# A two-block MoE transformer on one core: folded norms, token-major first heads, and embedding products inside the expert stretch

## The reference, cut to what matters

```python
o = _rmsnorm(o, subln_g) * (1.0 - lambda_init)         # o: (B, S, 8 heads, 128), first mixer
x = x + g1 * (o.reshape(B, S, D) @ w_out)
# second block, per layer
x = layer_norm(DEEPNORM_ALPHA * x + mix @ w_o[i], ln1_g[i], ln1_b[i])
ffn = expert_choice_moe(x, router_w[i], w1[i], w3[i], w2[i])
ple = jax.nn.sigmoid(x @ ple_gate_w[i] + ple_gate_b[i]) * (p[i] @ ple_w[i])
x = layer_norm(DEEPNORM_ALPHA * x + ffn + ple, ln2_g[i], ln2_b[i])
```

## Time and profile before

| | us |
|---|---|
| median of 3 runs (2154.5 to 2161.43) | 2156.48 |
| the profiled execution | 2149.18 |
| its span, first to last instruction | 2147.4 |
| TensorE busy | 1749.1 (81%) |
| VectorE busy | 445.4 (21%) |
| ScalarE busy | 399.9 (19%) |
| chain that ended last | PE 55%, DMA 35%, VectorE 4% |

### The profile page before, as it was taken

One profiled execution on the slowest core, in us unless ns is written; L12 is line 12 of the kernel. 1 busy time (PEld: TensorE's weight loads), 2 busy tenths in 40 slices (PEclk: granted clock), 3 DMA queues, 4 the chain that ended last, 5 costly groups with the idle time before them and its releaser, 6 DMA issues.

```text
span 2147.4 us, 31137 instructions
## 1 busy us (share of the span) xinstructions
PE 1749.1 (81%) x13297; PEld 1099.0 (51%) x13297; DVE 445.4 (21%) x1064; ACT 399.9 (19%) x911; POOL 0.6 (0%) x5
## 2 busy tenths in 40 slices
PE   6999999899899989899997565655799976565567
PEld 5868665568577655686743131211577541222114
DVE  3342211124633111225211000000244210000002
ACT  3141311122623111234211010000232310000001
POOL 0000000000000000000000000000000000000000
PEclk9999999999999999999998788887899988878869
DMA  9877899986737999944599999999924899999996
GB/s 358 280 272 270 340 387 376 391 255 196 265 138 316 367 395 394 337 153 141 184 409 421 422 421 421 421 421 421 349 99 169 326 412 421 421 422 421 421 421 282
DMA packets 185024, 716.00 MB, mean 333 GB/s; under 512 B 28428, under 2 KB 95928, under 8 KB 114360
## 3 DMA queue, kind: packets, MB, share of 16 engines
q1 hardware_dynamic: 184172, 713.48, 84.9%
q10 hardware_dynamic: 716, 0.53, 0.1%
HBM read 826.16 MB, written 1.05 MB: 385 GB/s over the span
## 4 chain that ended last, share of the span: by engine, by line
PE 55%; DMA 35%; DVE 4%; SPq 3%; ACT 2%; issue 1%; DVEq 0%; ACTq 0%
DMA ring<-in_w 28%; PE ps L1025 19%; PE ps L1472 7%; PE ps L1382 6%; DMA ring<-in_moe_w_up 5%; PE ps L1516 3%; PE ps L1392 3%; PE ps L1410 3%; PE ps L1366 2%; PE ps L1002 2%; PE ps L1164 1%; SPq L842 1%; DMA ring<-in_ada_w 1%; DMA ring<-in_moe_w_gate 1%; SPq L908 1%
## 5 line engine op out<-in xcount | busy, mean ns | idle before, releaser
L1472 PE MATMUL ps<-ring,ptb 128*32 128x512 f32 x1936 | 308.0, 783 | 207.3 <-DMA ring<-in_w 193.9
L1472 PEld LDWEIGHTS ps<-ring,ptb 128*32 128x32 f32 x1936 | 81.7, 138 | 419.7 <-issue 404.4
L1516 PE MATMUL ps<-ring,pb 128*32 128x512 f32 x1024 | 148.1, 734 | 73.8 <-DMA ring<-in_w 72.5
L1025 PE MATMUL ps<-xT,ring 128*128 128x256 f32 (+2 forms) x640 | 138.4, 385 | 1.0 <-ACT xT L1815 0.4
L1516 PEld LDWEIGHTS ps<-ring,pb 128*32 128x32 f32 x1024 | 39.1, 131 | 175.5 <-issue 172.9
L1025 PEld LDWEIGHTS ps<-xT,ring 128*128 128x128 f32 (+2 forms) x640 | 113.9, 185 | 26.3 <-issue 10.2
L2606 DVE TENSOR_TENSOR kT<-pb,ps 128x1024 f32<-128x1024 f32 x8 | 9.8, 1221 | 521.2 <-ACT pb L2005 521.2
L1025 PE MATMUL ps<-oT,ring 128*128 128x256 f32 x512 | 114.0, 381 | 2.0 <-DVE oT L2360 1.1
L1025 PE MATMUL ps<-hT,ring 128*128 128x256 f32 x480 | 106.3, 384 | 1.3 <-ACT hT L1815 1.3
L1382 PE MATMUL ps<-ring,vt 128*32 128x256 f32 x1536 | 92.9, 401 | 16.5 <-DMA ring<-in_moe_w_up 14.8
L1025 PEld LDWEIGHTS ps<-oT,ring 128*128 128x128 f32 x512 | 96.2, 190 | 15.6 <-DVE oT L2360 2.0
(11 more groups left out here) (473 smaller groups left out, 1916.5 us busy)
## 6 DMA issues: line engine op xcount, KB each, us to landing
ring<-in_w SPq DMA_DIRECT2D x370, 1024.0 KB
ring<-in_moe_w_gate SPq DMA_DIRECT2D x96, 1024.0 KB
ring<-in_moe_w_up SPq DMA_DIRECT2D x96, 1024.0 KB
ring<-in_moe_w_down SPq DMA_DIRECT2D x96, 1024.0 KB
ring<-in_ada_w SPq DMA_DIRECT2D x48, 1024.0 KB
ring<-in_diff_w_in SPq DMA_DIRECT2D x12, 1024.0 KB
ring<-in_w_o SPq DMA_DIRECT2D x8, 1024.0 KB
ring<-in_ple_gate_w SPq DMA_DIRECT2D x8, 1024.0 KB
```

Of the source, the lines that this page charges most:

```text
L1025: last = mmul(o, l, r, start=start, stop=stop)
L1472: last = mmul(ps[32 * j:32 * j + 32, 2 * a + h, :], xg[:, k, 32 * j:32 * j + 32], w[j][2 * k2 + h], start=(k == 0), stop=(k == C - 1))
L1516: last = mmul(ps[32 * j:32 * j + 32, 6 + h, :], hidT2[:, c, 32 * j:32 * j + 32], w[j][2 * c2 + h], start=(c == 0), stop=(c == C - 1))
```

## The change

- The value products of the first attention take the probabilities as weights, so a head's output is tokens by features (`h_tok`, the same memory as `oT`). ScalarE squares it per token with a running sum (`head_squares`), from step 3 on inside the loop. The root and the reciprocal run once for all heads, on 16 columns, VectorE scales 16 blocks, `turn_heads` transposes them, and ScalarE copies them with the gain into `qT`, from which the output projection reads. The last ada part of this attention moves from after step 5 to after step 7. `ada_columns` moves behind the transposes. A table load for roots stands ahead of the last move.
- In norms other than the first, `square_sum` writes 64 tokens into each quarter of the partitions; root and reciprocal run on 64 columns, and four products spread the result into bank 3, from which VectorE multiplies. Idle products: 2, the spreading, 2, where there were 8.
- In the second block's expert layers `hT`, a new buffer `extra` (it also holds `cpad`) and two rotary constant tables take two slots more of the first group (index 0). In layer 0 the constants are loaded again. Guests are awaited in three batches; guests 3 to 6 load after the last value product.
- The embedding inputs load inside group 0, are turned at the start of group index 1, and their four value jobs run in that group after the hidden transposes, into banks 0 to 3. VectorE multiplies them out of PSUM by the sigmoids. Their weights' slot stands between slots 31 and 32 of that group. Idle products replace them in `norm_router` (8) and `route2` (10 for 2). ALPHA goes into the first group's addition.

The diff, cut to its core:

```diff
-ADA_STEP = {"diff": (0, 1, 2, 3, 5), "nsa": (1, 5, 9)}
+ADA_STEP = {"diff": (0, 1, 2, 3, 7), "nsa": (1, 5, 9)}
...
-        cpad = sb("cpad", [P, C, 32])
+        extra = sb("extra", [P, 1536])
+        cpad = extra[:, 1280:1536].rearrange("p (k n) -> p k n", k=C)
...
+                  [tiles(hT, 0, 4), tiles(hT, 4, 4)],
+                  [extra[:, 0:1536], cst[:, CONST["cos_g"][0]:CONST["cos_g"][0] + 512]],
...
+        guest_batches = [range(0, 3), range(3, 7), range(7, 9)]
...
-                job(A["ple_w_2"][layer], 2, 1024, mm_T(pTb[layer], 2, [(256 * s, P, 0, 0), (256 * s + P, P, 0, T)]),
-                    copy_to((whole, pair_dst(hT, s))), new=(s == 0), last=(s == 3))
+                job(A["ple_w_2"][layer], 2, 1024, mm_T(hT[:, 2:4, :], 2, [(256 * s, P, 0, 0), (256 * s + P, P, 0, T)]),
+                    s, new=(s == 0), last=(s == 3), need=("pT_ready", layer + 1) if s == 0 else None,
+                    eng="dve", bank=s, own=True)
...
+                if (i, x) == (1, 32):
+                    ph[f"value{layer}"] = len(jobs)
+                    ple_value_jobs(layer)
...
-                          for r in half_rows], [slice(0, P)], out=oT[:, h, :])
+                          for r in half_rows], [slice(0, P)], out=h_tok[:, :, P * h:P * h + P])
...
-                load_guests(range(0, 3))
+                load_guests(guest_batches[0])
                 sp.wait_ge(S("v_done"), st_span[("mla", "gqa")[l]][-1]["n"] + 1)
-                load_guests(range(3, 5))
+                load_guests(guest_batches[1])
                 expert_slots(0, range(7, 11))
                 sp.wait_ge(S("tok_mm"), 2 * (2 + l) + 1)
-                load_guests(range(5, 7))
+                load_guests(guest_batches[2])
...
-                for i in range(1, E2_GROUPS):
+                expert_slots(1, range(0, 2))
+                sp.wait_ge(S("slot_used"), e2_slot[l, 0, 24] + 1)
+                sp.dma_start(hT[:, 0:2, :], A["p_2"][l, 0].rearrange("(a p) n -> p a n", p=P)).then_inc(S("p_in"), 16)
+                if l == 0:
+                    g0 = CONST["cos_g"][0]
+                    sp.dma_start(cst[:, g0:g0 + 512], A["consts"][:, g0:g0 + 512]).then_inc(S("consts_rest"), 16)
+                expert_slots(1, range(2, 32))
+                load_jobs(f"value{l}")
+                expert_slots(1, range(32, 48))
+                for i in range(2, E2_GROUPS):
...
-            for l in range(2):
-                sp.dma_start(yT[:, 4 * l:4 * l + 2, :], A["p_2"][l, 0].rearrange("(a p) n -> p a n", p=P))\
-                    .then_inc(S("p_in"), 16)
...
+                    if n == 0:
+                        last = mmul(ps[:, 2, 0:T], K("ones"), sq[:, T * c:T * c + T], start=(c == 0), stop=(c == C - 1))
+                        continue
+                    for j in range(4):
+                        last = mmul(ps[32 * j:32 * j + 32, 2, 0:64], K("ones")[:, 0:32],
+                                    sq[:, T * c + 64 * j:T * c + 64 * j + 64], start=(c == 0), stop=(c == C - 1))
...
-                    idle_products(7, 8)
+                    idle_products(7, 2)
+                    pe.wait_ge(S("spread_in"), 1 + plain(n))
+                    for j in range(4):
+                        last = mmul(ps[:, 3, 64 * j:64 * j + 64], ident[:, 32 * j:32 * j + 1].to_broadcast([P, P]),
+                                    st[:, 0:64], start=True, stop=True)
+                    last.then_inc(S("spread_mm"), 1)
+                    idle_products(7, 2)
...
+                    if x["kind"] == "diff":
+                        v = x["pairs"][0][2]
+                        for i, (tt, on) in enumerate(((0, 0), (1, 0), (1, 1))):
+                            last = mmul(ps[:, b, P * tt:P * tt + P], pt[:, 0, P * i:P * i + P], v[on],
+                                        start=on == 0, stop=on == tt, skip_group_check=True)
...
+                if len(xs) - 1 in ada:
+                    ada_other(ADA_X[name] + ada.index(len(xs) - 1))
+
+            def turn_heads(s):
+                pe.wait_ge(S("pn_done"), s + 1)
+                if s >= 2:
+                    pe.wait_ge(S("pn_sq"), s - 1)
+                for h, tt in itertools.product(range(2), range(TT)):
+                    at = P * (2 * s + h)
+                    last = tr(ps[:, 6 + s % 2, T * h + P * tt:T * h + P * tt + P], h_tok[:, tt, at:at + P])
+                last.then_inc(S("pn_mm"), 1)
...
-                project(span[f"value{m - 2}"][2:])
-                idle_products(4, 2)
+                idle_products(4, 10)
...
+                        if i == 1:
+                            pe.wait_ge(S("p_in"), 16 * (l + 1))
+                            for k in range(2):
+                                for tt in range(TT):
+                                    last = tr(ps[:, 7, T * k + P * tt:T * k + P * tt + P], hT[:, tt, P * k:P * k + P])
+                            last.then_inc(S("p_mm"), 1)
...
+                    if i == 1:
+                        project(span[f"value{l}"])
...
+                    if i == 1:
+                        await_need(pe, ("job", span[f"value{l}"][-1]))
...
-            pe.wait_ge(S("o_evac"), o_after["diff"])
+            for s in range(4):
+                turn_heads(s)
             ada_columns(range(0, 5), (2, 3, 4))
-            partition_norms(0)
-            pe.wait_ge(S("pn_done"), 4)
+            pe.wait_ge(S("pn_sq"), 4)
...
-                func(st[:, :], ps[:, 2, 0:T], ACT.Sqrt, bias=eps_col, scale=1.0 / D).then_inc(S("std_ready"), 1)
+                w = 64 if n else T
+                func(st[:, 0:w], ps[:, 2, 0:w], ACT.Sqrt, bias=eps_col, scale=1.0 / D).then_inc(S("std_ready"), 1)
...
+            def head_squares(h):
+                act.wait_ge(S("o_evac"), h + 1)
+                squared = (sqb if h < 4 else rt)[:, T * (h % 4):T * (h % 4) + T]
+                for tt in range(TT):
+                    last = func(squared[:, P * tt:P * tt + P], h_tok[:, tt, P * h:P * h + P], ACT.Square,
+                                accum_out=pn[:, 2 * h + tt:2 * h + tt + 1])
+                return last
...
+                    if name == "diff" and i >= 3:
+                        head_squares(i - 3)
+                if name == "diff":
+                    func(misc[:, 54:55], eps_col, ACT.Sqrt)
                 move(xs[-1])
+                if name == "diff":
+                    for h in range(5, 8):
+                        last = head_squares(h)
+                    link(last)
+                    func(pn[:, 0:16], pn[:, 0:16], ACT.Sqrt, bias=eps_col, scale=1.0 / P).then_inc(S("pn_std"), 1)
...
+            for s in range(4):
+                act.wait_ge(S("pn_mm"), s + 1)
+                func(pair_dst(qT, s), ps[:, 6 + s % 2, :], ACT.Copy, scale=coef[:, 2:3]).then_inc(S("pn_sq"), 1)
...
-                link(V.reciprocal(st[:, :], st[:, :]))
-                for ins in pairs(hT if n < 4 else xT, st[:, :], ALU.mult):
+                if n:
+                    V.reciprocal(st[:, 0:64], st[:, 0:64]).then_inc(S("spread_in"), 1)
+                    dve.wait_ge(S("spread_mm"), 1 + plain(n))
+                    by = ps[:, 3, 0:T]
...
+                for a, j in enumerate(span[f"value{l}"]):
+                    await_need(dve, ("job", span[f"gate{l}"][a]))
+                    dve.wait_ge(S(finished(j)[0]), finished(j)[1])
+                    V.tensor_tensor(vt[:, 512 * a:512 * a + 512], vt[:, 512 * a:512 * a + 512], ps[:, a, :], ALU.mult)\
+                        .then_inc(S("res_evac"), 1)
+                await_need(dve, ("job", span[f"value{l}"][3]))
                 for a in range(4):
-                    dve.wait_ge(S(evacuated(span[f"gate{l}"][a])[0]), evacuated(span[f"gate{l}"][a])[1])
-                    last = V.tensor_tensor(pair_dst(hT, a), pair_dst(hT, a), vt[:, 512 * a:512 * a + 512], ALU.mult)
-                link(last)
-                for a in range(4):
-                    last = V.scalar_tensor_tensor(pair_dst(xT, a), pair_dst(xT, a), ALPHA, pair_dst(hT, a),
-                                                  ALU.mult, ALU.add)
+                    last = V.tensor_tensor(pair_dst(xT, a), pair_dst(xT, a), vt[:, 512 * a:512 * a + 512], ALU.add)
...
-                        V.tensor_tensor(flat(xT), flat(xT), psf(0, 4), ALU.add).then_inc(S("y_added"), 1)
+                        V.scalar_tensor_tensor(flat(xT), flat(xT), ALPHA if i == 0 else 1.0, psf(0, 4),
+                                               ALU.mult, ALU.add).then_inc(S("y_added"), 1)
...
+            dve.wait_ge(S("pn_std"), 1)
+            V.reciprocal(pn[:, 0:16], pn[:, 0:16]).then_inc(S("pn_inv"), 1)
+            dve.wait_ge(S("pn_inv"), 1)
+            for s in range(4):
+                for h, tt in itertools.product((2 * s, 2 * s + 1), range(TT)):
+                    o = h_tok[:, tt, P * h:P * h + P]
+                    last = V.tensor_scalar(o, o, pn[:, 2 * h + tt:2 * h + tt + 1], None, ALU.mult)
+                last.then_inc(S("pn_done"), 1)
...
```

(10 more changed lines are left out.)

84 lines of the change are left out of this document (35 added, 49 removed).

## The result

The changed kernel takes 2137.88 us (median of 7 runs, 2133.21 to 2144.39) where the kernel before takes 2154.41 beside it (7 runs, 2150.23 to 2161.43): ratio 0.9929, 95% interval 0.9912 to 0.9947, so 15.3 us less (11.4 to 19.0); the plain medians are 16.5 apart. A second set gave 0.9936 (0.9922 to 0.9951). The forecast was 14.8 us less and a median of 2141.7, which is 3.8 above the measured one; 2.1 of that is the kernel before, whose median of three runs was 2156.48 when the forecast was made.

A forecast was written before the change was run, and what follows sets the result against it. DMA bytes were taken to bound the two expert stretches, the engines' chain the mixers. Terms -0.9 -7.5 -3.4 -3.0 = -14.8 us took the profiled 2149.2 to 2134.4; 7.3 more for the median gave 2141.7, range 2136 to 2147 (68%).

The forecast's parts named there:

- Start: Start of the kernel: eight transposes of the embedding inputs leave TensorE's chain, -0.9 us.
- Tail: End of the first attention: output projection starts at 167.2 instead of 174.77, -7.5 us, bounds -10 to -2.
- Norms: Three folded norms: shorter root and reciprocal on 64 columns, -1.1, -1.1 and -1.2, sum -3.4 us, bounds -5 to 0.
- eight instructions at 0.11: Folded norms: TensorE's spreading of the result, priced at 0.9 us.
- Expert layers: Second block's two expert layers: added guests less loads moved into the stretch, -1.2 and -1.8, sum -3.0 us.
- two slots are worth 5.0 us: Expert stretches: two more guests per layer save two slot loads of 2.52 us each, -5.0 us before what moved in.
- Rival 1: The clock falls at four re-made places, 1.9 us each: -7.2 us in all, 2149.3 us; chance 14%.
- Rival 2: Steps don't overlap: the first attention's end gives 2 us, norms nothing, -5.9 us, 2150.6 us; chance 8%.
- Rival 3: Expert layers, group 2: the ring runs dry, 10.7 us lost per layer, run slower; chance 5%.
- Rival 4: Expert stretches: DMA had slack and guests count in full, -10 for -3 us, 2134.7 us; chance 5%.

The follow-up runs named there:

- experts-only kernel: Kernel before with only the moved embedding values, two added guests and shorter start: 2149.53 us, ratio 0.9978.
- no idle: Changed kernel without the four covering products in each of its three folded norms: 2152.76 us, ratio 0.9982.
- best: Changed kernel plus an unused root before each later norm's squares, three idle products in the third folded norm, four in the first attention: 2134.09 us, ratio 0.9915.
- best2: The kernel called best plus three idle products in each of two TensorE waits at the second attention's start: 2138.17 us, ratio 0.9917.

## Why the prediction was right

The total was right, in part by luck: terms that were off, and stages that had no term, cancel.

**Start**, -0.9: the experts-only kernel has -0.8. The changed kernel's profiles have 2 us more there, which is the clock at 34 to 38 us and comes and goes with the same code.

**Tail**, -7.5: mis-sized, with the right mechanism. Profiles with the old tail have 45.9, 48.3 and 48.5 us, seven with the new one 37.9 to 39.8 (mean 39.0): 8.6 less. The steps held to within 0.7 us but for the ada part, and the profiles without a low clock in the ada part take 37.9 us, 8.0 less than 45.9. What was off is the row that it was measured against: before's own profile had the shortest of the three old tails; in the other two the ada part (4.70 and 4.46 us for 3.66) and the spreading of the roots (24 of its instructions took 4.50 in the earlier trace rows; all 32 take 5.74 there, 6.68 and 6.56 in the others) ran at a lower clock. The table load cost 1.30 us from its start to the next instruction's, as the earlier trace rows had it, not the 2.66 us of the Trainium skill ("ScalarE: Activation LUTs", "What ACT_TABLE_LOAD costs").

**Norms**, -3.4: too large. -0.8 each at the first two; at the third -0.9 in three profiles at the full clock, -0.3 in one, nothing in three where the clock fell, both of the changed kernel's among them. Two steps failed: "eight instructions at 0.11" took 1.10 us, not 0.9 (the hand-overs took 0.1 more as well), and the third norm was priced at the full clock. Against that the third mixer ran 1.7 us faster in four of seven profiles with the new norms, a gain that was in no term and whose cause isn't known.

**Expert layers**, -3.0: right, -1.4 and -2.2 by the means. That two slots are worth 5.0 us was right to within 1 us (5.7 and 6.0).

Together -0.8 -8.6 -1.6 -3.6 = -14.6, beside -15.3 measured. So the sum came out right with one term 1.1 too small, one 0.6 too small and one 1.8 too large. But this leaves out what had no term, again by means over the profiles (three with the old tail, seven with the new one, no idle and best's aside). The largest:

- From the second mixer's first projection to norm 2, the expert layer included, it took 419.8 to 423.1 us in the three profiles with the old tail and 424.5 to 429.7 in all eleven with the new one. By the means that is +4.8 us: 2.5 in the mixer, 2.3 in the routing and the expert layer.
- Out projection to norm 1: -1.8, within its spread of 5 to 6 us. Third mixer -1.0, fourth +0.2.

With these, and -0.4 for the third norm, the sum is -12.8 us, or -14.4 with the start as it came on average (-2.4). Both lie within the measured 11.4 to 19.0. So the forecast's rule that a microsecond of the mixers is a microsecond of the run isn't borne out stage by stage; whether the new tail is what lengthens the stages behind it isn't shown, and the run with the tail alone gained 11.8 us all the same.

**Rival 1**, the clock, was half true: it fell at the tail and at the third norm in both profiles of the changed kernel, and cost some 1.9 and 1 us there, not 7.2 in all. But it is as near as the run without idle products shows: 11 us where the four remaining products of each norm go too. **Rival 2** fell: the steps do overlap. **Rival 3** is a cliff that lies 7.7 us away, not 4. **Rival 4** fell with the run without guests.

The rule of the Trainium skill that I had set beside rival 1 ("TensorE: Matmul & The Clock Gate", "Part 1: The HAM clock gate": an idle TensorE goes back to half rate) agrees with no idle's windows, 0.50 and 0.53 behind waits that nothing covers (1.85 and 1.50 us at norm 1, 1.78 and 1.41 at norm 2).

**What stays open**: the second mixer took 82.0 to 83.0 us in the three profiles with the old tail and 83.0 to 86.1 in ten with the new (no idle aside), without an edit there. TensorE's clock in its attention differs, but best2 shows that covering the two waits doesn't mend it. Nor is it known what lengthens the routing and expert layer behind it, what else holds ada_six back, or why three runs without the covering products took no longer than the changed kernel.

## What to carry to other kernels

Split a change into its parts and read each stage in several profiles: one execution's tail was 2.5 us better than its like, and a sum made from it can be off by so much. Add up all stages, those that nobody touched too: here 5 us of the gain went back in them. Count covering products as part of the kernel: when a wait is shortened, some of the products that covered it can go (four of eight did at two norms; at the third the clock fell in four of seven profiles), but taking out the last four cost more than the shortened chain had given. Where a root or another function needs its own table, call it once, unused, while ScalarE waits anyway; the load of 1.28 us then stands on no path. A ring's slack can be worked out beforehand (slots times time per slot, from the last slot's landing) and it held to 1 us in one stretch and 3 in the other, with the products ahead priced at the clock that they really got; worked out from the kernel before, it was 3.7 us too small.

## What the runs showed of the hardware

The clock's cost lay mostly behind the place where it fell: without the covering products the second norm's spreading took 1.18 us for 1.10, and the mixer that followed lost 4 to 6 us. A clock fall can come again for several executions (17.10, 17.12, 17.10 us at the third norm in three executions of two kernels with the same norm) and yet be away in others with the same norm (16.16 without the two guests, 16.14 with 40 idle products in the stretch ahead). Whether such an edit far away is the cause isn't shown: at the tail and at the start it comes and goes with no edit ahead of it. The unused root itself took 0.20 us, and squares ran in its table without another load.
